# Attention values of branch A at other weight units, and transposed probabilities in six places instead of four, in a two-layer encoder on one core

## Chip, cores and metric

The kernel runs on one core of a Trainium2 chip. The metric is the device time of one execution in microseconds (us); the time of a kernel is the median over several executions. The core has five engines that run their own instruction streams and meet only through semaphores: TensorE (PE), VectorE (DVE), ScalarE (ACT), GpSimd (POOL) and SyncE (SP), which here only issues DMAs.

## What is computed

Two layers over 256 tokens of width 1024. In each, one projection `z` feeds three branches, whose gated sum passes `w_out`; then comes a SwiGLU channel mixer.

```python
h = rms_norm(x, norm_mix[l]);  z = h @ w_in[l]            # 6656 columns: qkv of A, qkv of B, pool channels, gates
ya = dense_gqa_blocked(qa, ka, va) @ w_branch_a[l]         # A: 8 query heads, softmax(q k^T) v over 256 keys
...
yb = ob.reshape(b, s, B_OUT_WIDTH) @ w_branch_b[l]         # B: 3 groups of 4 heads, windows of their own
yc = multiscale_pool(uc, pool_lin[l], pool_scale[l]) @ w_branch_c[l]   # C: pooling, then a linear map per group
merged = gates[:, :, 0] * ya + gates[:, :, 1] * yb + gates[:, :, 2] * yc
x = x + merged @ w_out[l]
x = x + (silu(h2 @ w_ffn_gate[l]) * (h2 @ w_ffn_up[l])) @ w_ffn_down[l]
```

## The kernel before

**Units.** All weights come as one stream of 68 units per layer, each 128 x 2048 float32 (1 MB), in a ring of four slots. Unit `t` is loaded into `w_raw` by SP once unit `t-4` is done, ACT rounds it to `w_hi` (line 751), DVE makes the rest `w_lo = w_raw - w_hi` (line 998), both two units ahead, and PE multiplies three passes: hi x hi (1319), hi x lo (1321), lo x hi (1330). Each pass is 128 x 512, four K tiles, for the two token halves m = 0 and 1, so an ordinary unit is 24 matmuls.

**What lies in front of a unit.** Units 0 to 25 are the projection, two units to a chunk of 512 columns (`z0` to `z12`). In front of a unit's matmuls PE may have other work: scores of two pairs of heads (lines 1410 and 1419) at units 10, 14, 18 and 22, and values, that is probabilities times v (line 1442), at 16, 20, 24 and 28. In the text, "pair p" is the p-th pair of the 16 softmax tiles, p = 0 to 7; values q takes pairs 2q and 2q+1; values 0 and 1 are branch A and end in banks `o0` and `o1`. Within a unit, between m = 0 and m = 1, come `pool` (1380) and the map of branch C, `mixed` (1386).

**PSUM banks.** Chunks `z7` to `z12` all use bank 0 for m = 0 and bank 1 for m = 1. The first matmul of the next chunk, at the even units 16, 18, 20, 22 and 24, therefore waits until DVE has taken the former chunk out of its bank. That is `take_gates` (line 1173, two instructions, m = 0 first), in DVE's program at the odd units 15 to 25. At 15 and 17 (`GATES_FIRST`) it stands ahead of the split of a weight unit, at the others behind it and behind the turns of that unit:

```python
if t in GATES_FIRST:
    take_gates(lay, t)
for j in splits_at(t):
    split(lay, j)
...
if t not in TURNS_FIRST:
    turns(lay, turns_within(t))
```

**The way of the probabilities.** ACT's exp and DVE's normalization make a pair; one unit later ACT splits them into halves (821), SP issues two DMA transposes (567) and, two units after that, POOL joins the halves (656) into `probsT` or `late_probs` (in the room of `rope`), where PE reads them. SP's program has the transposes of pair p ahead of a load of `w_raw`, and each of them waits for a join of pair p-1 (`probs_joined`). ACT's program at a unit is: split of a weight unit, split of probabilities, exp, join of heads (836, `JOINS_BEHIND`), turns (784 rounds an output `o` of values; DVE's 1053 makes its low part).

The engines have no scheduler: each stream is the order in which the loops over `t` are written, driven by these tables.

Of the kernel before, what the change touches and what calls it, by code (L numbers as in the profile page):

```python
# [31 lines left out]
NC = 512  # L32
# [9 lines left out]
RING = 4  # L42
# [10 lines left out]
UNITS = U_DOWN + 11  # L53
# [28 lines left out]
TURNED = len(REGIONS) * MT  # L82

JOINS_AHEAD = {8: [(1, 0), (1, 1)], 13: [(3, 0)]}
JOINS_BEHIND = {7: [(0, 0)], 10: [(0, 1)], 14: [(2, 0)], 15: [(4, 0)], 16: [(4, 1), (5, 0)], 17: [(3, 1)],
                18: [(2, 1), (5, 1)]}
JOIN_ORDER = [j for t in range(7, 19) for j in JOINS_AHEAD.get(t, []) + JOINS_BEHIND.get(t, [])]


# [27 lines left out]

TURNS_WITHIN = {
    0: [("mix_x", 2), ("mix_x", 3)],
    16: [("pool", 0)], 17: [("o", 0)], 18: [("pool", 1)], 20: [("o", 1)], 21: [("mixed", 0)], 23: [("mixed", 1)],  # L120
    24: [("o", 2)], 28: [("o", 3)], 30: [("merged", 0), ("merged", 1)],
    U_OUT + 3: [("ffn_x", 0), ("ffn_x", 1)], 
}

# [12 lines left out]
def quad_at(t, late):  # L137

    q, rest = divmod(t - PAIR_UNIT - late, 4)
    return q if 0 <= q < PAIRS // 2 and not rest else None  # L140
# [19 lines left out]

def turns_by_dma(t, lay=0):
    return [] if t == U_DOWN + 8 and lay == DEPTH - 1 else TURNS_BY_DMA.get(t, [])


def turns_before(t, lay=0):
# [91 lines left out]
def build(nc, x, stream, params, b_gate, eye, angles, pooling, mask, counts, out):  # L257
# [3 lines left out]
    with ExitStack() as ctx:  # L261
# [162 lines left out]
        def wait_joined(eng, lay, head):  # L424

            eng.wait_ge(heads_joined, lay * TURNED + JOIN_ORDER.index(head) + 1)
# [47 lines left out]

        def joined_probs(i):

            if i % 4 < 2:
                return probsT[:, i % 2, :]
            return late_probs[:, i % 2, :]

        def probs_part(i, j):

# [124 lines left out]
        def _(pool):  # L607
# [40 lines left out]
            def join_probs(lay, t, i):  # L648

                pool.wait_ge(probs_turned[i % 2], 16 * (lay * PAIRS + i // 2 + 1))  # L650
                if i == 2:
                    pool.wait_ge(rotated, (lay + 1) * TURNED)
                if i >= 4:
                    pool.wait_ge(unit_done, lay * UNITS + RING + t)
                both = joined_probs(i).bitcast(U16).rearrange("p (t h) -> p h t", h=2)
                nc.gpsimd.tensor_copy(both, probs_room(i).rearrange("p (h t) -> p h t", h=2)
                                      ).then_inc(probs_joined, 1)
# [644 lines left out]
        def _(pe):  # L1302
# [160 lines left out]
            for lay in range(DEPTH):  # L1463
                for t in range(UNITS):
# [3 lines left out]
                    if q is not None:  # L1468
                        scores(lay, 2 * q)
                        scores(lay, 2 * q + 1)  # L1470
                    q = quad_at(t, 6)
                    if q is not None:
                        values(lay, 2 * q)
                        values(lay, 2 * q + 1)
# [156 lines left out]
```

## Time and profile before

| | |
|---|---|
| Median of 3 runs | 802.65 us (802.24 to 803.89) |
| The profiled execution: its time / span of its trace | 802.35 / 800.5 us |
| PE busy | 794.4 us, 99% of the span |
| DVE / ACT / POOL busy | 72% / 61% / 29% |
| Granted TensorE clock over the span | 1.0 of full speed |
| Chain that ended last | 98% PE |

Times in the trace are counted from the start of the span. A row of the timeline is one instruction or several alike in a row: start, duration, engine, line, what it writes and reads, how many, and in brackets how long the engine was idle before it and what released it. A 128x512 matmul shows 0.39 us from start to end but the next one starts 0.23 us later, since they overlap; so starts are compared, not durations. The fp32 matmuls of scores, values and `mixed` appear as two records each. SPq is SP's DMA queue.

### The profile page before, as it was taken

Reading aid. Unit: us, or ns where it says so; the run is one execution under the profiler, and the core shown is the slowest. Engines: PE = TensorE matmul, PEld = TensorE weight load, DVE = VectorE, ACT = ScalarE, POOL = GpSimd, SP = SyncE. Lnnn points to the kernel's source line nnn. Section 1 sums busy time; section 2 is a strip of 40 time slices with the busy share of each in tenths; the row PEclk is TensorE's granted clock in tenths of the full one; section 3 lists DMA queues with packets and bytes.
Section 4 is the critical chain, followed back from the end, with each engine's and each line's share of the span. In section 5 each row is a group of like instructions: output and inputs, shape, how many; then the busy total and the mean of one; then the engine's idle time right before and its main releaser. Section 6 shows DMA issues by size and latency. Waiting matters only on the chain.

```text
span 800.5 us, 9766 instructions
## 1 busy us (share of the span) xinstructions
PE 794.4 (99%) x3768; PEld 652.1 (81%) x3768; DVE 579.5 (72%) x692; ACT 485.4 (61%) x554; POOL 234.4 (29%) x212
## 2 busy tenths in 40 slices
PE   8999999999999999999999999999999999999998
PEld 6888877888888888888888887878888888888886
DVE  6899977868676767655379989777686676676551
ACT  6778787673675445545557888866647645545420
POOL 1346622230014444430023316222200244444200
PEclk9999999999999999999999999999999999999999
DMA  9796898764677667676656887875746776687551
GB/s 335 287 249 200 212 257 245 211 224 165 205 235 226 201 223 215 207 254 207 202 197 195 235 220 217 251 237 180 233 169 198 233 239 201 219 233 217 195 209 50
DMA packets 109166, 173.89 MB, mean 217 GB/s; under 512 B 88608, under 2 KB 88768, under 8 KB 91712
## 3 DMA queue, kind: packets, MB, share of 16 engines
q1 hardware_dynamic: 106912, 165.96, 67.1%
q0 software_dynamic: 1920, 7.23, 2.6%
q8 instruction: 30, 0.49, 0.2%
q14 instruction: 16, 0.13, 0.1%
q10 hardware_dynamic: 288, 0.08, 0.0%
HBM read 150.96 MB, written 1.05 MB: 190 GB/s over the span
## 4 chain that ended last, share of the span: by engine, by line
PE 98%; DMA 1%; DVE 0%; ACT 0%; SPq 0%; issue 0%
PE bank L1319 31%; PE bank L1330 31%; PE bank L1321 31%; PE bank L1442 2%; PE bank L1419 1%; PE bank L1410 1%; PE bank L1352 1%; DMA x_sb<-in_x_dram 1%; PE bank L1380 0%; PE bank L1386 0%; DVE w_lo L998 0%; ACT w_hi L751 0%; ACT aT_hi L766 0%; PE bank L1452 0%; DVE scratch L1035 0%; DVE x_sb L1214 0%
## 5 line engine op out<-in xcount | busy, mean ns | idle before, releaser
L998 DVE TENSOR_TENSOR w_lo<-w_raw,w_hi 128x2048 fp32r<-128x2048 f32 x134 | 314.0, 2346 | 116.0 <-ACT w_hi L751 115.8
L751 ACT ACTIVATE w_hi<-w_raw 128x2048 fp32r<-128x2048 f32 x134 | 256.4, 1916 | 151.8 <-DMA w_raw<-in_stream_dram 151.7
L1319 PE MATMUL bank<-w_hi,aT_hi 128*128 128x512 f32 x832 | 326.6, 392 | 0.2 <-issue 0.2
L1321 PE MATMUL bank<-w_hi,aT_lo 128*128 128x512 f32 x832 | 324.1, 390 | 0.0
L1330 PE MATMUL bank<-w_lo,aT_hi 128*128 128x512 f32 x832 | 223.1, 390 | 0.2 <-DVE w_lo L998 0.2
L1319 PEld LDWEIGHTS bank<-w_hi,aT_hi 128*128 128x128 f32 x832 | 156.2, 188 | 36.6 <-issue 3.4
L1330 PEld LDWEIGHTS bank<-w_lo,aT_hi 128*128 128x128 f32 x832 | 155.7, 188 | 33.1 <-DVE w_lo L998 0.7
L1321 PEld LDWEIGHTS bank<-w_hi,aT_lo 128*128 128x128 f32 x832 | 156.2, 188 | 32.0
L680 POOL COPY halves<-hid 128x512 uint16<-128x512 uint16 x44 | 72.3, 1673 | 13.0 <-DVE hid L1291 13.0
L689 POOL COPY hT_raw<-turned 128x512 uint16<-128x512 uint16 x44 | 33.6, 809 | 124.1 <-DMA turned<-halves 124.1
L1319 PE MATMUL bank<-w_hi,hT_hi 128*128 128x512 f32 x176 | 68.5, 389 | 0.0
L1321 PE MATMUL bank<-w_hi,hT_lo 128*128 128x512 f32 x176 | 68.5, 389 | 0.0
L979 ACT ACTIVATE sg<-bank,rstd 128x256 f32<-128x256 f32 x44 | 20.8, 474 | 66.8 <-PE bank L1330 66.7
L1330 PE MATMUL bank<-w_lo,hT_hi 128*128 128x512 f32 x176 | 47.7, 389 | 0.0
L633 POOL TENSOR_TENSOR sx<-ssx 128x2 f32<-128x2 f32 x4 | 1.0, 255 | 158.5 <-ACT probsT L887 158.5
L1284 DVE SCALAR_TENSOR_TENSOR scratch<-bank,rstd,sg 128x256 f32<-128x256 f32 x44 | 20.9, 480 | 30.3 <-ACT sg L979 30.2
L1319 PEld LDWEIGHTS bank<-w_hi,hT_hi 128*128 128x128 f32 x176 | 33.0, 188 | 6.8
L1321 PEld LDWEIGHTS bank<-w_hi,hT_lo 128*128 128x128 f32 x176 | 33.0, 188 | 6.9
L1330 PEld LDWEIGHTS bank<-w_lo,hT_hi 128*128 128x128 f32 x176 | 33.0, 188 | 6.9
L629 POOL TENSOR_TENSOR rs<-rs_in,neg_half 128x8 f32<-128x8 f32 (+2 forms) x24 | 34.3, 1430 | 2.0
L627 POOL TENSOR_SCALAR rs_in<-ss 128x8 f32<-128x8 f32 (+2 forms) x24 | 8.5, 353 | 77.2 <-DVE ss L1089 76.6
L1048 DVE TENSOR_TENSOR hT_lo<-hT_raw,hT_hi 128x512 fp32r<-128x512 f32 x22 | 22.9, 1042 | 8.2 <-ACT hT_hi L771 8.2
(118 smaller groups left out, 807.6 us busy)
## 6 DMA issues: line engine op xcount, KB each, us to landing
w_raw<-in_stream_dram SPq DMA_DIRECT2D x135, 1024.0 KB, 5.0
bias_sb<-in_b_gate_dram POOLq DMA_DIRECT2D x12, 256.0 KB, 4.8
par<-in_params_dram POOLq DMA_DIRECT2D x3, 384.0 KB, 5.4
w_raw<-in_stream_dram SPq DMA_DIRECT2D x4, 256.0 KB, 5.0
head_halves<-in_pooling_dram POOLq DMA_DIRECT2D x1, 1024.0 KB, 6.1
zqk<-in_counts_dram POOLq DMA_DIRECT2D x2, 512.0 KB, 4.5
out_dram<-x_sb SPq DMA_DIRECT2D x4, 256.0 KB, 4.2
x_sb<-in_x_dram SPq DMA_DIRECT2D x2, 256.0 KB, 4.4
```

The lines of the kernel that those rows point to most:

```text
L629: nc.gpsimd.tensor_tensor(dst[0], dst[1], dst[2], ALU.pow).then_inc(signal, 1)
L680: nc.gpsimd.tensor_copy(halves[:, b, :, h, :], both[:, :, :, h]).then_inc(halves_ready, 1)
L689: nc.gpsimd.tensor_copy(both[:, :, :, :, h], turned[:, b, :, h, :, :].rearrange("p m k t -> p k m t")).then_inc(raw_ready, 1)
L751: nc.scalar.activation(w_hi[:, j % RING, :, :].rearrange("p k n -> p (k n)"), w_raw[:, j % RING, :, :].rearrange("p k n -> p (k n)"), ACT. ...
L979: nc.scalar.activation(sg[:, i % 2, m, :], B((f"f{i}", m))[:, 0:256], ACT.Sigmoid, scale=rstd[:, 1, m:m + 1]).then_inc(sig_done, 1)
L998: nc.vector.tensor_tensor(w[0], w[1], w[2].bitcast(F32), ALU.subtract).then_inc(unit_lo, 1)
L1048: nc.vector.tensor_tensor(turn_dest(name, False), raw, hi, ALU.subtract).then_inc(hidden_ready, 1)
L1284: made.append(link(nc.vector.scalar_tensor_tensor(scratch[:, 2 * NC + 256 * m:2 * NC + 256 * m + 256], B((f"f{i}", m))[:, 0:256], rstd[:, ...
L1319: nc.tensor.matmul(o, src[0][:, k, tok], w_hi[:, slot, wk + i, :], start=first and i == 0, stop=False)
L1321: nc.tensor.matmul(o, src[1][:, k, tok], w_hi[:, slot, wk + i, :], start=False, stop=False)
L1330: last = nc.tensor.matmul(o, src[0][:, k, tok], w_lo[:, slot, wk + i, :], start=False, stop=final and i == len(tiles) - 1)
L1442: last = nc.tensor.matmul(B(("o", o))[HD * r:HD * r + HD, at:at + w], zvu[:, kt, col(r):col(r) + HD], joined_probs(2 * p + r)[:, c:c + cw] ...
```

## The change

Values 0 and 1 move on PE from units 16 and 20 to 18 and 22, behind the scores there; values 2 and 3 stay. The turns of `o0` and `o1` move from 17 and 20 to 19 and 22, those of `mixed` from 21 and 23 to 23 and 24. The joined probabilities get a third room (pairs 2 and 5) in `zqk[:, 1, 0:1024]`, whose heads must have been joined by ACT first; for that, the join of heads (2, 1) moves on ACT from unit 18 to 17. POOL's join of a pair no longer waits for the end of the unit before it, but for the values that last read the room, and for pair 2 for the joins of heads (3, 1) and (2, 1).

```diff
-JOINS_BEHIND = {7: [(0, 0)], 10: [(0, 1)], 14: [(2, 0)], 15: [(4, 0)], 16: [(4, 1), (5, 0)], 17: [(3, 1)],
-                18: [(2, 1), (5, 1)]}
+JOINS_BEHIND = {7: [(0, 0)], 10: [(0, 1)], 14: [(2, 0)], 15: [(4, 0)], 16: [(4, 1), (5, 0)], 17: [(3, 1), (2, 1)],
+                18: [(5, 1)]}
...
-    16: [("pool", 0)], 17: [("o", 0)], 18: [("pool", 1)], 20: [("o", 1)], 21: [("mixed", 0)], 23: [("mixed", 1)],
-    24: [("o", 2)], 28: [("o", 3)], 30: [("merged", 0), ("merged", 1)],
+    16: [("pool", 0)], 18: [("pool", 1)], 19: [("o", 0)], 22: [("o", 1)], 23: [("mixed", 0)],
+    24: [("o", 2), ("mixed", 1)], 28: [("o", 3)], 30: [("merged", 0), ("merged", 1)],
...
+def values_at(t):
+
+    return {18: 0, 22: 1, 24: 2, 28: 3}.get(t)
...
-            if i % 4 < 2:
-                return probsT[:, i % 2, :]
-            return late_probs[:, i % 2, :]
+            room = i // 2 % 3
+            if room == 2:
+                return zqk[:, 1, NC * (i % 2):NC * (i % 2) + NC]
+            return (probsT, late_probs)[room][:, i % 2, :]
...
-                if i >= 4:
-                    pool.wait_ge(unit_done, lay * UNITS + RING + t)
+                if i in (4, 5):
+                    wait_joined(pool, lay, (3, 1))
+                    wait_joined(pool, lay, (2, 1))
+                if i >= 6:
+                    wait_full(pool, lay, ("o", (i // 2 - 3) // 2))
...
-                    q = quad_at(t, 6)
+                    q = values_at(t)
```

**PE where unit 20 begins.** The rows are the last passes of unit 19 (bank 1) and the first of unit 20 (bank 0, chunk `z10`). Before:

```order
L1319 MATMUL bank1<-w_hi,aT_hi 128x512
L1321 MATMUL bank1<-w_hi,aT_lo 128x512
L1330 MATMUL bank1<-w_lo,aT_hi 128x512 x4
L1442 MATMUL bank3<-probsT,zvu 64x256 x4
L1442 MATMUL bank3<-rope,zvu 64x256 x4
L1319 MATMUL bank0<-w_hi,aT_hi 128x512
L1321 MATMUL bank0<-w_hi,aT_lo 128x512
```

And with the change:

```order
L1328 MATMUL bank1<-w_hi,aT_hi 128x512
L1330 MATMUL bank1<-w_hi,aT_lo 128x512
L1339 MATMUL bank1<-w_lo,aT_hi 128x512 x4
L1328 MATMUL bank0<-w_hi,aT_hi 128x512
L1330 MATMUL bank0<-w_hi,aT_lo 128x512
```

The eight matmuls of values are gone from between the units; the same has happened where unit 16 begins.

**DVE from unit 17 to unit 20.** The `gates` rows are `take_gates`, the `w_lo` rows the splits of units 19, 20, 21. Before:

```order
L1173 SCALAR_TENSOR_TENSOR gates<-bank,rstd,bias_sb 128x512 x2
L998 TENSOR_TENSOR w_lo<-w_raw,w_hi 128x2048
L1053 TENSOR_TENSOR oT_lo<-bank,oT_hi 128x4x128
...
L998 TENSOR_TENSOR w_lo<-w_raw,w_hi 128x2048
...
L998 TENSOR_TENSOR w_lo<-w_raw,w_hi 128x2048
L1173 SCALAR_TENSOR_TENSOR gates<-bank,rstd,bias_sb 128x512 x2
```

With the change:

```order
L1182 SCALAR_TENSOR_TENSOR gates<-bank,rstd,bias_sb 128x512 x2
L1007 TENSOR_TENSOR w_lo<-w_raw,w_hi 128x2048
...
L1007 TENSOR_TENSOR w_lo<-w_raw,w_hi 128x2048
...
L1007 TENSOR_TENSOR w_lo<-w_raw,w_hi 128x2048
L1062 TENSOR_TENSOR oT_lo<-bank,oT_hi 128x4x128
L1182 SCALAR_TENSOR_TENSOR gates<-bank,rstd,bias_sb 128x512 x2
```

The low part of `o0` has moved between the split of unit 21 and the gates of chunk `z9`.

**ACT at units 17 to 19.** `w_hi` rows are the splits of units 19, 20 and 21, the `qkT<-zqk` rows joins of heads. Before:

```order
L751 ACTIVATE w_hi<-w_raw 128x2048
L821 ACTIVATE scratch<-probs 128x1024 x2
L836 ACTIVATE qkT<-zqk 128x2x4x128
L784 ACTIVATE oT_hi<-bank 128x4x128
L751 ACTIVATE w_hi<-w_raw 128x2048
L809 ACTIVATE probs,den<-probs,neg_max 128x512 x2
L836 ACTIVATE qkT<-zqk 128x2x2x128 x2
L789 ACTIVATE pooledT<-bank 128x512
L751 ACTIVATE w_hi<-w_raw 128x2048
L821 ACTIVATE qkT<-probs 128x1024 x2
```

With the change:

```order
L760 ACTIVATE w_hi<-w_raw 128x2048
L830 ACTIVATE scratch<-probs 128x1024 x2
L845 ACTIVATE qkT<-zqk 128x2x4x128
L845 ACTIVATE qkT<-zqk 128x2x2x128
L760 ACTIVATE w_hi<-w_raw 128x2048
L818 ACTIVATE probs,den<-probs,neg_max 128x512 x2
L845 ACTIVATE qkT<-zqk 128x2x2x128
L798 ACTIVATE pooledT<-bank 128x512
L760 ACTIVATE w_hi<-w_raw 128x2048
L830 ACTIVATE qkT<-probs 128x1024 x2
L793 ACTIVATE oT_hi<-bank 128x4x128
```

The second join, that of heads (2, 1), has come to unit 17, and the rounding of `o0` stands behind the split of pair 4 at unit 19.

## Rows read from the trace of the kernel before

**Rows 1.** The page, busy time (us), share of the span and instructions

```profile
PE 794.4 (99%) x3768; PEld 652.1 (81%) x3768; DVE 579.5 (72%) x692; ACT 485.4 (61%) x554; POOL 234.4 (29%) x212
```

**Rows 2.** Waits of PE: us in total, times, longest us

```profile
PE bank L1330 <- DVE w_lo L998: 0.2, 1, 0.2
```

**Rows 3.** Timeline of PE, layer 0, units 15 to 17

```profile
101.03 1.07 PE L1330 MATMUL bank<-w_lo,aT_hi 128*128 128x512 f32 x4
102.03 1.08 PE L1442 MATMUL bank<-probsT,zvu 128*64 128x256 f32 x8
...
103.91 0.50 PE L1319 MATMUL bank<-w_hi,aT_hi 128*128 128x512 f32 x1
...
109.55 1.07 PE L1330 MATMUL bank<-w_lo,aT_hi 128*128 128x512 f32 x4
110.46 0.39 PE L1319 MATMUL bank<-w_hi,aT_hi 128*128 128x512 f32 x1
```

**Rows 4.** Timeline of DVE, the gates of z7 in layers 0 and 1

```profile
102.03 1.40 DVE L1173 SCALAR_TENSOR_TENSOR gates<-bank,rstd,bias_sb 128x512 f32<-128x512 f32 x2
...
495.65 1.40 DVE L1173 SCALAR_TENSOR_TENSOR gates<-bank,rstd,bias_sb 128x512 f32<-128x512 f32 x2
```

**Rows 5.** Timeline of PE, layer 0, end of unit 19 and start of 20

```profile
129.03 1.07 PE L1330 MATMUL bank<-w_lo,aT_hi 128*128 128x512 f32 x4
130.03 1.08 PE L1442 MATMUL bank<-probsT,zvu 128*64 128x256 f32 x8
...
131.91 0.50 PE L1319 MATMUL bank<-w_hi,aT_hi 128*128 128x512 f32 x1
```

**Rows 6.** Timeline of DVE, layer 0: low part of o0, split of unit 21, gates of z9

```profile
120.10 0.69 DVE L1053 TENSOR_TENSOR oT_lo<-bank,oT_hi 128x512 fp32r<-128x512 f32 x1 [0.92 <-ACT oT_hi L784]
...
128.57 2.29 DVE L998 TENSOR_TENSOR w_lo<-w_raw,w_hi 128x2048 fp32r<-128x2048 f32 x1 [2.14 <-ACT w_hi L751]
130.78 1.41 DVE L1173 SCALAR_TENSOR_TENSOR gates<-bank,rstd,bias_sb 128x512 f32<-128x512 f32 x2
```

**Rows 7.** Timeline of ACT: layer 0, units 17 to 19; layer 1, units 14 to 19

```profile
114.56 1.92 ACT L751 ACTIVATE w_hi<-w_raw 128x2048 fp32r<-128x2048 f32 x1 [0.53 <-DMA w_raw<-in_stream_dram]
...
118.27 1.36 ACT L836 ACTIVATE qkT<-zqk 128x1024 uint16<-128x1024 uint16 x1
119.49 0.58 ACT L784 ACTIVATE oT_hi<-bank 128x512 fp32r<-128x512 f32 x1
...
126.62 1.92 ACT L751 ACTIVATE w_hi<-w_raw 128x2048 fp32r<-128x2048 f32 x1 [1.59 <-DMA w_raw<-in_stream_dram]
...
490.03 0.80 ACT L836 ACTIVATE qkT<-zqk 128x512 uint16<-128x512 uint16 x1
...
511.03 0.57 ACT L784 ACTIVATE oT_hi<-bank 128x512 fp32r<-128x512 f32 x1
...
519.73 1.92 ACT L751 ACTIVATE w_hi<-w_raw 128x2048 fp32r<-128x2048 f32 x1 [2.43 <-DMA w_raw<-in_stream_dram]
```

**Rows 8.** POOL's joins of probabilities: ns min/median/max, first and last start

```profile
L656 POOL COPY probsT<-zqk x8: 1359/1367/3060, 137.8 to 562.0; 128x1024 uint16<-128x1024 uint16 x8
```

**Rows 9.** Timeline of SP's queue: first transpose of pair 3, layers 0 and 1

```profile
117.44 1.24 SPq L567 DMA_TRANSPOSE gates<-scratch  x1
...
508.99 1.23 SPq L567 DMA_TRANSPOSE gates<-scratch  x1
```

**Rows 10.** Timeline of PE, layer 1, the last passes of units 15 and 19

```profile
494.77 1.07 PE L1330 MATMUL bank<-w_lo,aT_hi 128*128 128x512 f32 x4
...
522.77 1.07 PE L1330 MATMUL bank<-w_lo,aT_hi 128*128 128x512 f32 x4
```

**Rows 11.** Windows: us, PE busy (x), ..., granted clock, DMA share, GB/s; first two: warm-up matmuls

```profile
2.90:3.40 0.50, 0.50 (x7) 0.50 (x7) 1.00 0.67 182
...
7.40:7.90 0.50, 0.50 (x12) 0.50 (x10) 1.00 0.84 217
...
797.00:800.50 3.50, 0.13 (x1) 0.00 (x0) 0.69 (x1) 0.00 (x0) 0.00 (x0) 0.96 0.19 75
```

## The prediction, on record before the change ran

> **What bounds the kernel now.** I read the page first: PE is busy for 794.4 of 800.5 us [rows 1]. Then the waits of PE: none in the body is over 0.2 us [rows 2]. So PE is the bound from end to end, and every microsecond that PE waits or works more is added to the time. A change pays only through work of PE; it costs wherever it uncovers a wait that is hidden now. So I went through the timelines at the places where the change alters what PE has in front of a unit, and asked each time who must have finished.
>
> Ordinary passage between units: the four last passes start at 109.55 and the next unit starts 0.91 us later [rows 3], 0.2275 a pass. With values in front of unit 16, its first matmul starts at 103.91 instead of 101.03 + 0.91 = 101.94: values take 1.97 us [rows 3]. At unit 20 it is 131.91 against 129.94, the same [rows 5].
>
> **The change on PE.** It has the same matmuls. In each layer values 0 and 1 now stand behind scores, twice, so instead of two inserts with an entry and an exit each there is one longer insert. The 16 records of values need 16 x 0.114 (half of a 512-column pass) = 1.82 us, so 0.15 of the 1.97 is entry and exit; the entry alone is 0.09 (101.94 to 102.03). A merge saves nothing at the least, and at most both inserts' 0.15, 0.3 in all. I take 0.1 for each of the four merges, since scores and values still differ in tile shape and there is one change between them: **-0.4 us** (0 to -1.2). The Trainium skill has a rule for this (TensorEngine Tiling (Array Packing), Key Properties): changing the tiling mode drains the engine, using another tile of the same mode doesn't. By it a merge removes one of four drains, by the trace's 0.09 at entry about 0.1 each, which is what I took.
>
> **What the values covered.** Chunks z7 to z12 share banks 0 and 1, so an even unit can't start until DVE has taken the former chunk's m = 0 out of bank 0. Where values or scores stand in front, PE has 2 us of other work meanwhile. The change takes that cover from units 16 and 20 and doubles it at 18 and 22, where it is not needed.
>
> *Unit 16.* DVE takes z7 at 102.03 in layer 0 and 495.65 in layer 1, two instructions in 1.40 us, the first done after about 0.70 [rows 4]: 102.73 and 496.35. DVE's program up to there is untouched. PE is ready at 101.94 and at 494.77 + 0.91 = 495.68 [rows 10]. Waits: 0.79 and 0.67, **+1.5 us**. Behind it on PE is everything.
>
> *Unit 20.* DVE takes z9 at 130.78, right behind the split of unit 21, which starts at 128.57 because that unit's weights came late (ACT idle 1.59 for a DMA, DVE 2.14 for ACT) [rows 6, 7]. Now values at 130.03 to 131.91 hide it [rows 5]. With the change PE wants bank 0 at 129.94 + 0.79 - 0.1 = 130.63, and three things stand in the way:
>
> 1. The gates stay behind the split of 21 (19 is not in GATES_FIRST).
> 2. The turn of o0 has moved in between. ACT rounds o0 at unit 19 behind the split of pair 4: from the start of a w_hi to the end of that split are 118.27 - 114.56 = 3.71, the turn is 0.58 [rows 7], DVE's low part 0.69 [rows 6], the first gates 0.70. So bank 0 is free 3.71 + 0.58 + 0.69 + 0.70 = 5.68 us after the weights of unit 21 land.
> 3. Those weights land later. On SP the load of unit 21 is queued behind the transposes of pair 3, and these wait for the join of pair 2. That join now waits for ACT's join of heads (2, 1), which comes behind that of (3, 1): it starts where the turn of o0 started, 119.49, and takes the 0.80 of its size: 120.29 [rows 7]. One join of probabilities by POOL is 1.36 [rows 8]: 121.65. Now the first transpose starts at 117.44 [rows 9], so SP is 4.2 us later, and behind it are the second transpose and the loads of units 21 and 22. From first transpose to landing were 126.62 - 117.44 = 9.18: it lands at 130.83 instead of 126.62.
>
> Bank 0 is free at 130.83 + 5.68 = 136.51, PE is ready at 130.63: **5.9 us**. In layer 1: ACT's turn starts at 511.03, + 0.80 + 1.36 = 513.19; from transpose to landing 519.73 - 508.99 = 10.74 [rows 7, 9], landing 523.93, bank free 529.61; PE is ready at 522.77 + 0.91 + 0.67 - 0.1 = 524.25 [rows 10]: **5.4 us**.
>
> *Other places.* At 18 and 22 PE has scores and values, 4 us, in front; unit 22 comes 11 us after unit 20 and its gates stand right behind the split of 23, nothing between, so I charge nothing. If the weights of 23 lag by as much as those of 21, some 2 us of cover still remain. `mixed` has the same length inside a unit as before, and what needs it, unit 26, comes over a unit later: nothing. If its turns ran into the gates of z12, C's first unit would wait, by at most the 2.3 us of a split. POOL's joins of pairs 3 to 7 lose a wait for PE; nobody on the path waits for them: nothing. The new w_lo of unit 21 is ready before PE gets there, because PE itself is held.
>
> *Clock.* At the end of the program the granted clock is 1.00 until PE has been idle for some time: PE ends 0.13 into the window from 797.0, and the mean of 0.96 over 3.5 us says the lower level (half, 1.2 of 2.4 GHz) for 0.28 us, so the clock fell about 3.1 us after the last matmul [rows 11]. Both waits at unit 20 are longer than that, and PE has no wait like them now. At the start the warm-up matmuls come 7 per half microsecond, later 12 [rows 11], so the low rate lasted there for at least the 2.5 us from 0.9 to 3.4. In low clock half of the time is lost, 1.25 us at least for a fall; a fall may also come in one wait and not the other. I take **+2 us** (0 to 4) for both layers. The skill (TensorE: Matmul & The Clock Gate, Part 1) calls the throttled state the default that activity releases, and idleness brings back; by it both waits would be followed by slow matmuls, +2.5 or more where I count 2.
>
> **Sum.** -0.4 + 1.5 + 5.9 + 5.4 + 2 = +14.4 us on the profiled execution's 802.35 (span 800.5): 816.7. The median of the runs shown is 0.3 above that execution: 817.0.
>
> **Bounds.** Low: merges save 1.2, the weights of 21 land as now (126.62 and 519.73), bank 0 free at 132.30 and 525.41, waits 1.7 and 1.2, no fall: +3.2, 805.9. High: 10.74 from transpose to landing in layer 0 too (+1.6), both joins at the 3.06 us maximum instead of 1.36 [rows 8] (+3.4), a clock fall at both (+2): 824.
>
> **Rivals.**
>
> - *Long waits and the clock falls* (my forecast): 817.0, between 814 and 821. 0.50.
> - *Long waits, the clock holds*: 815.0, between 810 and 817. For it: an idle PE of 5.4 to 5.9 us is not far above 3.1, and no row shows a fall inside the run. 0.31.
> - *Only the order on DVE counts*, the SP chain doesn't lengthen: if transposes of pair 3 really drain while loads do, the weights of 21 are as early as now. Waits 1.7 + 1.2 + 1.5, minus 0.4: +4.0, 806.6. Against it: the join of pair 2 can't start before ACT is done with (2, 1), and ACT's row has no slack there. 0.10.
> - *More than that*: a further wait appears at unit 22 or 24 because weights of 23 and 25 lag too, 822 and above. For it: every late landing delays ACT's split of the next pair, which delays the next transposes. 0.05.
> - *The other side: not slower.* The joins of pairs 3 and later are freed from the wait for a unit's end; if that let SP and so the weights run ahead, DVE would take z9 by 130.6, PE would lose only the 1.5 at unit 16, and the merges give 0.4 to 1.2 back: 802.9 to 803.7, within 0.2%. It decides at a landing of unit 21 at 130.63 - 5.68 = 124.95 or earlier, 1.7 us before today's, while the only join ahead of that load gets later. If also DVE were early at unit 16, the merges alone would be left: 801.4 to 802.6. 0.03 for no change, 0.01 for faster.
>
> **How the numbers follow.** A difference under 0.2% (1.6 us) can't be told from none here. The first two cases hold 0.81 and share the mechanism; the time is that of the likelier, 817.0. The range 809 to 822 leaves out the third case, the fourth and the last: 0.19. Slower by over 0.2%: the first four, 0.96; same 0.03; faster 0.01.
>
> **What would show it.** Timeline of PE in the changed kernel: a gap of 0.7 to 0.8 us before unit 16 and one of 5 to 6 before unit 20, in both layers, both released by DVE's gates, and none over 0.3 elsewhere. SP's queue: the first transpose of pair 3 some 4 us later than [rows 9], ACT's wait for the weights of unit 21 longer by as much. DVE's row: w_lo, oT_lo, gates in this order, with DVE idle before oT_lo for about 1.4 us. The granted clock below 1.00 in the windows behind the long gaps. The merged inserts are 0.1 shorter than the two apart. The prediction is wrong if PE's gaps at unit 20 are under 3 us, which would mean step 3 fails, or if the gap is there but the time is made up behind it: since PE never waits now, nothing could give it back.

## The result, and the profile after

The changed kernel takes 822.7 us (median of 5 runs, 820.9 to 824.1) against 803.4 (802.2 to 803.9) for the kernel before: 1.0243 times the time. Brackets behind such a ratio are its 95% interval, here [1.0232, 1.0253]. Slower was forecast, at 817.0, with a range of 809 to 822: the direction is right, and the time lies above the range. The profiled execution has a span of 820.1 us against 800.5, and all of the 19.6 us but 0.6 is time in which PE waits or runs at its lower clock.

First the page's busy times, then the waits of PE (us in total, times, longest), which answer to [rows 1] and [rows 2]:

```profile
PE 800.5 (98%) x3768; PEld 657.4 (80%) x3768; DVE 586.4 (72%) x692; ACT 485.0 (59%) x554; POOL 228.9 (28%) x212
```

```profile
PE bank L1328 <- DVE gates L1182: 14.2, 3, 7.5
```

PE has the same 3768 matmuls and 6.1 us more busy time: slower matmuls, not more of them. In the body of the kernel the waits over 0.2 us are three, all on the gates. The timeline of PE shows where (answers to [rows 5] and [rows 10]): the end of unit 19 and the first matmul of unit 20 in layer 0, then unit 15 to 16 and unit 19 to 20 in layer 1.

```profile
129.43 1.07 PE L1339 MATMUL bank<-w_lo,aT_hi 128*128 128x512 f32 x4
136.85 0.79 PE L1328 MATMUL bank<-w_hi,aT_hi 128*128 128x512 f32 x1 [6.35 <-DVE gates L1182]
...
504.38 1.07 PE L1339 MATMUL bank<-w_lo,aT_hi 128*128 128x512 f32 x4
505.84 0.50 PE L1328 MATMUL bank<-w_hi,aT_hi 128*128 128x512 f32 x1 [0.40 <-DVE gates L1182]
...
532.90 1.07 PE L1339 MATMUL bank<-w_lo,aT_hi 128*128 128x512 f32 x4
541.47 0.79 PE L1328 MATMUL bank<-w_hi,aT_hi 128*128 128x512 f32 x1 [7.49 <-DVE gates L1182]
```

Counted from the last passes with the 0.91 us of an ordinary passage, the waits before unit 20 are 136.85 - 129.43 - 0.91 = 6.5 and 7.7 us, the one before unit 16 is 0.55 in layer 1. Their cause stands in the timelines of ACT, DVE, POOL and SP of layer 0, which answer to [rows 6, 7, 9]:

```profile
116.16 1.98 ACT L845 ACTIVATE qkT<-zqk 128x1024 uint16<-128x1024 uint16 x2
...
131.12 1.91 ACT L760 ACTIVATE w_hi<-w_raw 128x2048 fp32r<-128x2048 f32 x1 [8.18 <-DMA w_raw<-in_stream_dram]
...
134.84 0.57 ACT L793 ACTIVATE oT_hi<-bank 128x512 fp32r<-128x512 f32 x1
```

```profile
133.07 2.29 DVE L1007 TENSOR_TENSOR w_lo<-w_raw,w_hi 128x2048 fp32r<-128x2048 f32 x1 [7.97 <-ACT w_hi L760]
135.44 0.69 DVE L1062 TENSOR_TENSOR oT_lo<-bank,oT_hi 128x512 fp32r<-128x512 f32 x1
136.05 1.40 DVE L1182 SCALAR_TENSOR_TENSOR gates<-bank,rstd,bias_sb 128x512 f32<-128x512 f32 x2
```

```profile
118.30 2.64 POOL L665 COPY zqk<-gates 128x1024 uint16<-128x1024 uint16 x2 [13.62 <-ACT qkT L845]
120.85 0.55 POOL L671 DMA_DIRECT2D zqk<-in_counts_dram  x1
```

```profile
119.73 2.59 SPq L573 DMA_TRANSPOSE gates<-scratch  x2
122.38 3.03 SPq L596 DMA_DIRECT2D w_raw<-in_stream_dram  x2
```

The chain is the one that was named: ACT's joins of heads, which end at 118.14, release POOL's join of pair 2 (POOL was idle for 13.62 us before it), that releases SP's transposes at 119.73, the weights of unit 21 are queued behind them, ACT and DVE stand idle for them for 8 us, and DVE splits, turns o0 and only then takes the gates that PE needs. In a row of windows stand the stretch, its length, the busy time of PE, PE's weight loads, DVE, ACT and POOL (with instructions), and then the granted clock, the last column but two:

```profile
135.00:136.00 1.00, 0.00 (x0) 0.00 (x0) 0.92 (x2) 1.00 (x2) 0.00 (x0) 0.92 0.95 218
...
137.00:142.00 5.00, 5.00 (x12) 3.93 (x13) 5.00 (x6) 1.73 (x5) 3.12 (x3) 0.50 0.84 287
142.00:143.00 1.00, 1.00 (x4) 0.76 (x4) 1.00 (x1) 0.87 (x1) 0.00 (x0) 0.67 0.10 37
538.00:539.00 1.00, 0.00 (x0) 0.00 (x0) 1.00 (x1) 1.00 (x2) 0.00 (x0) 0.81 0.00 0
539.00:545.00 6.00, 3.53 (x8) 2.81 (x9) 5.92 (x9) 4.35 (x7) 2.37 (x3) 0.50 0.77 197
545.00:546.00 1.00, 1.00 (x5) 0.78 (x4) 1.00 (x1) 0.00 (x0) 0.76 (x1) 0.78 1.02 418
```

0.92 over 135 to 136 means 0.16 us at the lower level (1.2 of 2.4 GHz), so the clock fell at 135.84; 0.67 over 142 to 143 puts its return at 142.66. In layer 1 it was low from 538.62 to 545.44. Unit 20, which takes 5.44 us at full clock, took 8.31 and 7.41: 2.9 and 2.0 us lost, which is half of the time for which the clock was still low after PE had started again.

The balance: 6.5 + 7.7 (unit 20) + 4.9 (clock) + 0.55 (unit 16) + 0.6 (a later start, unit 15's last passes start at 101.63 instead of 101.03) - 0.4 (four merges) = 19.9, against 19.6.

### The profile page after: what moved, and what is told of

The parts are those of the page before. It is cut to its first block, busy times and chain, and to the rows that moved or that the text cites. A ratio compares the mean times of both kernels' runs of the same rounds, so it can differ in the third digit from the quotient of the medians.

```text
span 820.1 us, 9766 instructions
## 1 busy us (share of the span) xinstructions
PE 800.5 (98%) x3768; PEld 657.4 (80%) x3768; DVE 586.4 (72%) x692; ACT 485.0 (59%) x554; POOL 228.9 (28%) x212
## 4 chain that ended last, share of the span: by engine, by line
PE 86%; DMA 5%; DVE 3%; ACT 2%; issue 2%; POOL 1%; SPq 1%; ACTq 0%; DVEq 0%; POOLq 0%
PE bank L1328 27%; PE bank L1330 27%; PE bank L1339 27%; DMA w_raw<-in_stream_dram 4%; PE bank L1451 2%; DVE w_lo L1007 1%; PE bank L1361 1%; PE bank L1428 1%; ACT w_hi L760 1%; SPq L573 1%; DVE probs L1168 1%; DMA x_sb<-in_x_dram 1%; POOL probsT L665 1%; ACT scratch L830 0%; ACT qkT L830 0%
## 5 line engine op out<-in xcount | busy, mean ns | idle before, releaser
L1007 DVE TENSOR_TENSOR w_lo<-w_raw,w_hi 128x2048 fp32r<-128x2048 f32 x134 | 319.1, 2384 | 118.6 <-ACT w_hi L760 118.3
L689 POOL COPY halves<-hid 128x512 uint16<-128x512 uint16 x44 | 69.0, 1599 | 13.0 <-DVE hid L1300 13.0
L698 POOL COPY hT_raw<-turned 128x512 uint16<-128x512 uint16 x44 | 35.3, 849 | 126.0 <-DMA turned<-halves 126.0
```

The costliest lines, as they stand in the source:

```text
L689: nc.gpsimd.tensor_copy(halves[:, b, :, h, :], both[:, :, :, h]).then_inc(halves_ready, 1)
L698: nc.gpsimd.tensor_copy(both[:, :, :, :, h], turned[:, b, :, h, :, :].rearrange("p m k t -> p k m t")).then_inc(raw_ready, 1)
L1007: nc.vector.tensor_tensor(w[0], w[1], w[2].bitcast(F32), ALU.subtract).then_inc(unit_lo, 1)
```

## The experiments

The kernel before, run beside them, took 802.9 us with the first four, 803.3 with the next four, 803.4 with the three after these and 802.9 with the last. The question: the forecast named two causes that work together, the order on DVE (gates behind the late split and the turn of o0) and the late weights, and a third term that follows, the clock. Which has to be undone?

**Gates ahead at unit 19.**

```diff
-GATES_FIRST = (15, 17)
+GATES_FIRST = (15, 17, 19)
```

> The changed kernel with DVE's take_gates of chunk z9 ahead of the split of unit 21 (19 added to GATES_FIRST), nothing else. Theory (PE waits at unit 20 for bank 0, which DVE empties behind a split whose weights are late): DVE reaches the gates at about 125 us of layer 0, z9's m = 0 is full at 127.6, so bank 0 is free before unit 19 ends; both waits at unit 20 (6.5 and 7.7 us) and the low clock behind them (4.8 us) go: 822.7 - 19.0 = 803.7, at most 1 us more if the split of unit 21, now behind the gates, becomes late. Rival (PE waits for the weights of unit 21 or for a join, and DVE's gates are only named by the profile): the wait moves to unit 21 or 22 and the time stays above 812.

Measured: 811.3 us, 1.0106 [1.0088, 1.0124], a miss for the theory and for the rival. The waits before unit 20 are gone, as the theory says, but PE now waits before unit 22, 1.55 us in layer 0 and 3.7 in layer 1, with a fall of the clock behind the second; 0.91 before unit 16 of layer 1 and 0.33 before unit 24 are left besides:

```profile
546.29 0.80 PE L1328 MATMUL bank<-w_hi,aT_hi 128*128 128x512 f32 x1 [3.72 <-DVE gates L1182]
```

So 11 of 19 us hang on that one place, and the same pattern waits one chunk on: the gates of z10 at unit 21, behind the split of unit 23. The "2 us of cover" that I saw at unit 22 held only as long as PE itself was held up at unit 20.

**The turn of o0 back at 20.**

```diff
-    16: [("pool", 0)], 18: [("pool", 1)], 19: [("o", 0)], 22: [("o", 1)], 23: [("mixed", 0)],
+    16: [("pool", 0)], 18: [("pool", 1)], 20: [("o", 0)], 22: [("o", 1)], 23: [("mixed", 0)],
```

> The changed kernel with the turn of o0 at unit 20 instead of 19, nothing else: the gates of z9 stand right behind the split of unit 21 again, as before the change. Theory: of the 6.5 and 7.7 us at unit 20 the turn made DVE idle until ACT had split pair 4 and rounded o0, and 0.69 for the low part: bank 0 is free 0.8 us earlier by the changed kernel's own rows (w_lo ends at 135.36, gates start at 136.05 and 0.61 of it is the turn), so waits of 5.8 and 6.9, the clock still falls in both: 821.5. What I wrote before counted 1.4 us of DVE idle besides; the trace shows 0.08. Rival (the turn is a main part of the wait, and the clock holds with a shorter wait): below 817.

Measured: 822.0 us, 1.0238 [1.0221, 1.0255], near what was expected, with waits of 6.2 and 7.5 instead of 5.8 and 6.9. The rows of layer 0 show the gain and why it isn't seen in the waits:

```profile
132.54 1.91 ACT L760 ACTIVATE w_hi<-w_raw 128x2048 fp32r<-128x2048 f32 x1 [8.22 <-DMA w_raw<-in_stream_dram]
```

```profile
136.69 1.40 DVE L1182 SCALAR_TENSOR_TENSOR gates<-bank,rstd,bias_sb 128x512 f32<-128x512 f32 x2
```

Bank 0 is free 136.69 + 0.70 - 132.54 = 4.85 us after the landing instead of 5.63, as expected, but this time the weights landed 0.6 us later against PE, in layer 1 0.7. So the turn ahead of the gates is the small part, 0.8 us of each wait; the split behind late weights is the large one.

**Joins of heads one unit earlier.** In the other direction, the weights: ACT joins heads (3,1) and (2,1) at unit 16, so that POOL's join, the transposes and the weights behind them come earlier.

```diff
-JOINS_BEHIND = {7: [(0, 0)], 10: [(0, 1)], 14: [(2, 0)], 15: [(4, 0)], 16: [(4, 1), (5, 0)], 17: [(3, 1), (2, 1)],
+JOINS_BEHIND = {7: [(0, 0)], 10: [(0, 1)], 14: [(2, 0)], 15: [(4, 0)], 16: [(4, 1), (5, 0), (3, 1), (2, 1)],
```

> The changed kernel with ACT's joins of heads (3, 1) and (2, 1) at unit 16, nothing else. Theory (the join of pair 2 waits for the joins of heads, SP's transposes of pair 3 for that, and the weights of unit 21 for those): POOL joins pair 2 before ACT has split pair 3, the first transpose of pair 3 starts at about 116.3 instead of 119.7 in layer 0, the weights of unit 21 land at 126.5 to 127.7 instead of 131.1; the waits at unit 20 are 2.5 to 3.1 and 3.5 to 4.5 us, the clock falls in one of them at most: 809 to 814. Rival (DMA bandwidth, not the queue order, makes the weights late): the landing stays within 1 us of 131 and the time at 821 to 823.

Measured: 810.7 us, 1.0093 [1.007, 1.0116]. The time is in the expected range, but the two waits came out otherwise than expected (3.4 and 0.9 us instead of 2.5 to 3.1 and 3.5 to 4.5). The first transpose starts at 117.61 in layer 0, 2.1 us earlier than in the changed kernel, and the weights land 2.1 us earlier; in layer 1 they land 8.3 us earlier, 3.7 us ahead of unit 19's last passes, where the kernel before has 3.0 (two rows of ACT, layers 0 and 1, and PE before unit 20 of layer 1):

```profile
129.02 1.92 ACT L760 ACTIVATE w_hi<-w_raw 128x2048 fp32r<-128x2048 f32 x1 [5.23 <-DMA w_raw<-in_stream_dram]
...
527.41 1.92 ACT L760 ACTIVATE w_hi<-w_raw 128x2048 fp32r<-128x2048 f32 x1 [2.74 <-DMA w_raw<-in_stream_dram]
```

```profile
531.15 1.07 PE L1339 MATMUL bank<-w_lo,aT_hi 128*128 128x512 f32 x4
533.14 0.50 PE L1328 MATMUL bank<-w_hi,aT_hi 128*128 128x512 f32 x1 [0.92 <-DVE gates L1182]
```

That a change of ACT's order alone gives 12 us back shows that most of the late landing comes through that join. Layer 1 shows one thing more: with weights that are on time, the gates behind the split and the turn cost 0.9 us, without any values in front of unit 20.

**The places alone.** Values and turns back where they were; the six places and the waits of POOL that go with them stay.

```diff
-return {18: 0, 22: 1, 24: 2, 28: 3}.get(t)
+return {16: 0, 20: 1, 24: 2, 28: 3}.get(t)
...
-    16: [("pool", 0)], 18: [("pool", 1)], 19: [("o", 0)], 22: [("o", 1)], 23: [("mixed", 0)],
-    24: [("o", 2), ("mixed", 1)],
+    16: [("pool", 0)], 17: [("o", 0)], 18: [("pool", 1)], 20: [("o", 1)], 21: [("mixed", 0)], 23: [("mixed", 1)],
+    24: [("o", 2)],
```

> The changed kernel with values 0 and 1 back at units 16 and 20 and the turns of o0, o1 and mixed where they were before; the six places, the changed waits of POOL and the earlier join of heads (2, 1) stay. It tells the cover from the chain. Theory (both count): PE has values in front of unit 20 again, which hides 2 us, but the weights of unit 21 still come some 4 us late through the chain of joins, so PE waits 3 to 5 us for bank 0 at unit 20, or for the join of pair 3 ahead of values 1; the wait at unit 16 is gone: 810 to 817 with the clock falling in one or both. Rival (only the position of the values matters): within 0.3% of the kernel before, 801 to 805.

Measured: 817.4 us, 1.0185 [1.017, 1.02]; the timeline of PE, layer 0:

```profile
133.50 1.08 PE L1451 MATMUL bank<-probsT,zvu 128*64 128x256 f32 x8 [1.54 <-POOL probsT L665]
...
139.29 0.80 PE L1328 MATMUL bank<-w_hi,aT_hi 128*128 128x512 f32 x1 [4.70 <-DVE gates L1182]
```

The first row is a wait of its own: values 1 wait for POOL's join of pair 3. In layer 1 there is one wait, 4.88 us before unit 20, and the clock falls in both layers. With the cover of 2 us back, the new places, with the join that has to wait for ACT, still cost 14.5 us, just above the range of the theory. Values taken away from units 16 and 20 are the smaller part of the loss, 5.3 us.

**Both repairs**, `GATES_FIRST = (15, 17, 19)` and the joins at unit 16:

> Both of the two repairs: gates of z9 ahead of the split of unit 21, and ACT's joins of heads (3, 1) and (2, 1) at unit 16. Theory (late weights of unit 21 and 23 through the chain of joins are one cause, the place of the gates behind a split the other, and each repair alone leaves the other's wait): no wait at units 20 and 22, only 0.5 to 1 us a layer at unit 16, the clock stays at 1.00, the merges give 0.4 back: 803 to 804.5, no difference to the kernel before that can be told. Rival (something else is late as well): a wait over 1 us stays and the time is above 806.

Measured: 808.7 us, 1.0055 [1.0035, 1.0074]. A miss for the theory that these two repairs are enough: PE waits 3.03 us before unit 24 and 0.57 before unit 22 in layer 0, with a fall of the clock behind the first, and 0.77 before unit 16 in layer 1.

**And the gates of z7 ahead of the pooled low halves.** The last kernel with, at unit 15 of DVE,

```diff
-                    if t == U_LOW:
-                        for m in range(MT):
-                            low_pooled(lay, m)
                     if t in GATES_FIRST:
                         take_gates(lay, t)
+                    if t == U_LOW:
+                        for m in range(MT):
+                            low_pooled(lay, m)
```

> As the kernel with both repairs, and at unit 15 DVE's gates of z7 ahead of low_pooled. Theory: z7's m = 0 is full at the middle of unit 15, DVE takes it 1.3 us earlier, so the wait at unit 16 (0.4 to 1.0 us a layer) goes: 0.5 to 1.5 us under the kernel with both repairs, 802 to 803, which the merges alone put 0.4 us below the kernel before. Rival (low_pooled, now behind the second gates and so behind the end of unit 15, makes PE wait in the pooling of unit 16): no gain over the kernel with both repairs.

Measured: 806.8 us (12 runs, 803.4 to 810.2), 1.0038 [1.0021, 1.0054], where 802 to 803 was expected. The wait before unit 16 is gone, as the theory says; one is left, 2.70 us before unit 24 of layer 0. DVE's timeline shows the pattern a third time: z11's gates at unit 23 stand behind the split of unit 25, whose weights are late, and behind the turn of `mixed` 0, which the change put at unit 23.

```profile
155.75 2.29 DVE L1007 TENSOR_TENSOR w_lo<-w_raw,w_hi 128x2048 fp32r<-128x2048 f32 x1 [3.44 <-ACT w_hi L760]
157.96 0.87 DVE L1031 SCALAR_TENSOR_TENSOR scratch<-bank,par,zqk 128x256 f32<-128x256 f32 x2
159.52 1.78 DVE L1053 TENSOR_TENSOR mixT_lo<-scratch,mixT_hi 128x512 fp32r<-128x512 f32 x1 [0.69 <-ACT mixT_hi L775]
161.23 1.40 DVE L1182 SCALAR_TENSOR_TENSOR gates<-bank,rstd,bias_sb 128x512 f32<-128x512 f32 x2
```

**Gates ahead up to unit 21, nothing else**: `GATES_FIRST = (15, 17, 19, 21)`.

> The changed kernel with take_gates ahead of the split at 15, 17, 19 and 21; the late joins stay. It tells whether late weights cost by themselves. Theory: with z9 and z10 taken ahead of the splits, PE no longer waits for bank 0 at 20 and 22, and the weights of unit 23 (low part ready at about 146.4 in layer 0, needed at 150) are late for DVE but not for PE: 803 to 805.5. Rival (late weights reach PE anyway): a wait of 1 us or more for w_hi or w_lo at unit 21 to 24, or for the gates at 24, and a time above 807.

Measured: 816.0 us, 1.0148 [1.012, 1.0176]. A clear miss: no wait before units 20 and 22, but 4.27 and 4.34 us before unit 24, with the clock falling in both layers (the row is layer 0), and 0.92 before unit 16 and 0.70 inside unit 23 in layer 1. With two places of the pattern repaired the kernel is slower than with one (811.3), since the wait that is handed on is longer and brings two falls of the clock instead of one.

```profile
163.19 0.79 PE L1328 MATMUL bank<-w_hi,aT_hi 128*128 128x512 f32 x1 [4.27 <-DVE gates L1182]
```

**The clock by itself.** The changed kernel with 42 small matmuls of no use (84 records) ahead of unit 20, so that PE is not idle while it waits.

```diff
+                    if t == 20:
+                        wait_free(pe, lay, ("o", 1))
+                        for _ in range(42):
+                            nc.tensor.matmul(B(("o", 1))[0:MT * HEADS, 0:MT * HEADS],
+                                             neg_half[:, :, :].rearrange("p m h -> p (m h)"),
+                                             neg_half[:, :, :].rearrange("p m h -> p (m h)"), start=True, stop=True)
```

> The changed kernel with 42 matmuls of 68 x 68 constants, about 0.14 us each, ahead of unit 20 into bank 3, which holds nothing then and whose content nothing reads: extra work of 5.9 us in the place of the wait of 6.5 and 7.7 us. Theory (the clock falls because PE idles, and the lower level after the wait costs 2.9 and 2.0 us): the waits for the gates shrink to about 0.6 and 1.8, the granted clock stays at 1.00, units 20 take 5.5 us again, and the kernel with 5.9 us more work a layer is 4.8 us faster than the changed one: 818. Rival (the slow matmuls after the wait have another cause, such as the DMA traffic in that stretch): the time stays at 822 to 824.

Measured: 817.4 us, 1.0164 [1.0138, 1.0191]. The timeline of PE and, behind it, the windows over both places:

```profile
131.16 5.34 PE L1483 MATMUL bank<-neg_half 128*68 128x68 f32 x84
138.40 0.50 PE L1328 MATMUL bank<-w_hi,aT_hi 128*128 128x512 f32 x1 [1.90 <-DVE gates L1182]
```

```profile
128.00:146.00 18.00, 16.10 (x132) 14.07 (x131) 11.22 (x13) 9.75 (x11) 4.49 (x4) 1.00 0.77 238
528.00:546.00 18.00, 16.97 (x136) 14.79 (x135) 11.39 (x14) 10.26 (x11) 4.50 (x4) 1.00 0.76 245
```

Unit 20 still starts late, by 138.40 - 130.26 - 0.91 = 7.2 us in layer 0 (6.5 in the changed kernel) and 6.4 in layer 1 (7.7), together 0.6 us less. The clock stays at 1.00, and the median falls by 5.3 us. The two profiled executions can be set side by side: PE's last passes come 5.1 us earlier than in the changed kernel, although this execution had started 0.8 us later (unit 15's last passes at 102.46 instead of 101.63). Of these 5.9 us, 0.6 are the earlier units 20, 0.55 is the wait before unit 16 of layer 1, which this execution doesn't have, and 4.8 are left for the clock, against the 4.9 read from the trace. So the slow matmuls behind the wait come from PE's idleness and not from what else moves there.

**The counts at unit 19.** In the kernel before, POOL issues the 512 KB load of the counts at 114.70, ahead of the transposes (117.44). In the changed kernel it follows them, at 120.85 (by 1.1 us), and moves beside them and the weights.

```diff
-                    if t == 17:
+                    if t == 19:
                         load_counts(lay)
```

> The changed kernel, with the load of the counts (and what it writes) issued by GpSimd at unit 19 instead of at unit 17. In the changed kernel that load is issued at 120.85 us in layer 0, between the transposes of pair 3 (119.73) and the landing of unit 21's weights (131.12); there the way from the transposes to the landing took 11.4 us, in the kernel before 9.2, and in layer 1 (which has the load at the same place) 10.8 against 10.7. Theory A, the load lengthens the way of the transposes and the weights in layer 0: 9.2 us again, the wait before unit 20 of layer 0 falls from 6.35 to about 4.3, the time from 822.7 to about 820.5. Theory B, the 2.2 us come from something else (what happens to be moving on the other queues): the wait stays within 0.7 of 6.35 and the time within 1 us of 822.7.

Measured: 820.0 us, 1.0203 [1.0188, 1.0219]. From SP's first transpose to the landing, layer 0:

```profile
121.08 2.59 SPq L573 DMA_TRANSPOSE gates<-scratch  x2
```

```profile
130.55 1.91 ACT L760 ACTIVATE w_hi<-w_raw 128x2048 fp32r<-128x2048 f32 x1 [6.32 <-DMA w_raw<-in_stream_dram]
```

That is 9.5 us where the changed kernel has 131.12 - 119.73 = 11.4 and the kernel before has 9.2; in layer 1 it is 9.3 against 10.8. PE's waits before unit 20 fall to 4.5 and 5.9, as the first theory says. The load of the counts, 1.1 us behind the first transpose, had cost 1.5 to 1.9 us of each landing: a DMA on POOL's queue lengthened a chain on SP's. The Trainium skill says (Trainium Kernel Development and Optimization, Key Constraints) that DMAs issued from different queues run on the same 16 engines and interleave. This run agrees.

The other kernels with the load at that place (gates ahead at 19, up to 21, at all five units of the changed kernel; the turn at 20; the places alone; the filled wait) bear it out: in their 12 layers the way took 10.5 to 12.5 us. But a load ahead of the transposes is no guarantee of the short way. The kernel before has it 2.7 us ahead in layer 0, where the way is 9.2 us, and 1.9 us ahead in layer 1, where it is 10.7; with the same order in the kernel before, below, it is 0.5 and 1.1 us ahead, and the way takes 11.1 and 10.7.

**Gates ahead at all five units.** The kernel with both repairs and the order at unit 15, and `GATES_FIRST = (15, 17, 19, 21, 23)`.

> The kernel with joins at unit 16, gates ahead of the pooled low halves at unit 15 and gates ahead of the split at units 15, 17 and 19 (806.8 us; its only wait of TensorE was 2.70 us before unit 24 of layer 0, on the gates that VectorE takes at unit 23 behind the late split of unit 25), with the gates ahead of the split at units 21 and 23 too. Theory A, the waits of TensorE come from nothing but gates behind a late split or turn, and the splits themselves have room: no wait over 0.5 us before units 16 to 26, TensorE's clock stays at 1.00, and the time is that of the kernel before, 802.5 to 804. Theory B, the splits have no room left for 1.4 us more: a wait on w_lo appears before unit 23 or 25, or on the turns before unit 24, of 1 to 4 us, and 806 to 810 us come out.

Measured: 802.6 us (12 runs, 802.2 to 804.6), 0.999 [0.9982, 0.9999]. No wait of PE over 0.2 us on anything that this change touches, clock 1.00 throughout (windows over both layers' places):

```profile
90.00:190.00 100.00, 100.00 (x546) 81.16 (x545) 72.93 (x93) 70.90 (x86) 29.98 (x22) 1.00 0.77 219
440.00:620.00 180.00, 180.00 (x911) 146.54 (x910) 147.00 (x198) 128.18 (x158) 47.48 (x37) 1.00 0.74 216
```

ACT still waits 4.70 us for the weights of unit 21 in it. The 0.1% (0.7 us) below the kernel before is of the size of the four merges (0.4 us), at the edge of what can be told.

**The same order in the kernel before.** Is the repair free by itself? The kernel before, with the gates ahead at unit 15 and at 19.

> The kernel before, values at units 16 and 20 and four places, with the gates ahead of the pooled low halves at unit 15 and ahead of the split at unit 19: the part of the repair that lies on VectorE, without the change. Theory A, the repair costs nothing itself and has nothing to gain where no gates are late (the kernel before has no wait over 0.5 us there): within 0.5 us of 803.3. Theory B, the moved splits cost something in both kernels (w_lo later before unit 21, the turns later): 804.5 to 807 us, and then a part of what is left of the loss in the repaired kernels is the repair's own.

Measured: 806.6 us, 1.004 [1.0026, 1.0053]. It costs 3.2 us there, by one wait of 1.60 us in each layer, in front of values at unit 16 (layer 1):

```profile
500.11 1.08 PE L1442 MATMUL bank<-probsT,zvu 128*64 128x256 f32 x8 [1.60 <-DVE mixT_lo L1129]
```

Values 0 at unit 16 need bank 3, which the pooled low halves at unit 15 set free. With values at unit 18 nobody waits for them so early. So my second theory was right in size and wrong in place: it is not the split but the low halves. And the order at unit 15 that helps the changed kernel is one that the kernel before could not have had for nothing.

**One line.** The changed kernel with `GATES_FIRST = (15, 17, 19, 21, 23)` and nothing else.

> The changed kernel with one line altered: gates ahead of the split at units 15, 17, 19, 21 and 23. The joins stay at units 16 and 17, so the weights of unit 21 still land late (ScalarE waited 8.2 and 8.1 us for them), and at unit 15 the pooled low halves stay ahead of the gates. With the gates ahead at units 15 to 21 alone it was 816.0, with waits of 4.27 and 4.34 us before unit 24, 0.92 before unit 16 of layer 1 and 0.70 before the insert of unit 23. Theory A, only the place of the gates on VectorE matters and the late weights still come in time for the matmuls that read them: no wait before unit 24, the clock holds, about 1 us is left before unit 16 and 0 to 1 before unit 23, and the time is 803 to 805. Theory B, the late weights need the joins moved as well: a wait on w_lo, on the turns or on the gates of 2 us or more in at least one layer, and 807 to 814.

Measured: 805.6 us (12 runs, 803.9 to 809.8), 1.0042 [1.0024, 1.0059]. It is 0.6 us above the range of the first theory, and no wait is over 1.0 us. This run tells the causes apart, by one row of ACT in layer 0:

```profile
131.19 1.92 ACT L760 ACTIVATE w_hi<-w_raw 128x2048 fp32r<-128x2048 f32 x1 [8.62 <-DMA w_raw<-in_stream_dram]
```

The weights land as late as in the changed kernel (131.12), and unit 20 doesn't wait at all. What is left are 1.0 and 0.3 us before `mixed` inside unit 23, for DVE's low part of o1, and 0.67 before unit 16 of layer 1:

```profile
154.05 1.13 PE L1395 MATMUL bank<-pooledT,par 128*128 128x256 f32 x4 [1.00 <-DVE oT_lo L1062]
```

These are 2.0 us in the profiled execution, which took 804.7, 1.8 above the kernel before. The median is 2.7 above it: four of the 12 runs lie above 809, and what they waited for no profile shows.

## Where the forecast held, and the step that failed

The direction and the mechanism were forecast; the time came out 5.7 us higher, above the range, and the clock term is the largest part of that.

*PE bounds the kernel, and nothing gives a wait back*: right. Apart from 0.6 us of a later start, every microsecond of the 19.6 is a wait or lower clock.

*Merges -0.4*: right in size. In the timeline of PE the merged insert of unit 18 takes 3.92 us:

```profile
113.49 1.07 PE L1339 MATMUL bank<-w_lo,aT_hi 128*128 128x512 f32 x4
114.49 2.02 PE L1428 MATMUL bank<-qkT 64*128 64x256 f32 x24
116.44 1.08 PE L1451 MATMUL bank<-probsT,zvu 128*64 128x256 f32 x8
117.36 1.03 PE L1451 MATMUL bank<-rope,zvu 128*64 128x256 f32 x8
118.32 0.50 PE L1328 MATMUL bank<-w_hi,aT_hi 128*128 128x512 f32 x1
```

118.32 - 113.49 - 0.91 = 3.92, where values alone took 1.97 and scores alone, by the same reading at unit 18 of the kernel before, 2.05: 0.10 saved.

*Unit 16, +1.5*: too much. It waited only in layer 1, 0.55 (up to 0.96 in the other kernels with this order). In layer 0 DVE came to the gates at 101.49, when PE's last passes had started at 101.63; in [rows 3, 4] the gates start 1.0 us behind the last passes.

*Unit 20, +5.9 and +5.4*: the mechanism is right at each link, the sizes were 6.5 and 7.7. In layer 0 two errors cancelled. The first transpose came 2.3 us later and not 4.2 (119.73 against 117.44, with PE itself 0.4 later), since ACT's split of unit 19 started at 112.44 instead of 114.56, and the joins behind it with it; and the way to the landing took 11.4 instead of 9.18. That the sum fits nevertheless is luck. The second step is where a part of the change was overlooked: behind the join that now waits stands POOL's load of the counts, which the change carries from ahead of the transposes to behind them; the run with the counts at unit 19 measured it. In layer 1 the links before the chain were late too: ACT rounds the weights of unit 19 at 517.70 behind 3.02 us of waiting for them, 1.5 us later against PE than before, and everything behind shifts with it. I had taken ACT's row up to there from the kernel before. Why those weights land later in layer 1 no run shows.

The sum behind the landing (5.68) was met: 136.75 - 131.12 = 5.63. But two roads of the same length lead there. ACT is done with the turn of o0 at 134.84 + 0.57 = 135.41, DVE with the split at 133.07 + 2.29 = 135.36, and the low part starts at 135.44. DVE was idle for under 0.1 us before it, where the forecast said 1.4. Its own rows don't give 1.4 either: in [rows 6, 7] DVE's split ends 1.95 + 2.29 = 4.24 us after the landing, against 3.71 + 0.58 = 4.29 for ACT's turn.

*Clock, +2*: this is the step that failed. The term was mis-sized: it measured 4.9 by the rows and 4.8 by the filled wait, outside the 0 to 4 that was given to it. A fall was priced at 1.25 us, half of the 2.5 us of low rate among the warm-up matmuls of [rows 11] (where the granted clock column itself shows 1.00), with room for the clock to fall only once. In the changed kernel both waits had a fall, the low stretches lasted 6.8 us and not 2.5, and each cost half of what was left of it after PE started again, 2.9 and 2.0. With +4.9 in its place the sum is 819.9. The second term that was too small is the wait of layer 1, 7.7 instead of 5.4, which brings it to 822.2; the 1.0 us too much at unit 16 and the 0.6 of a later start nearly cancel.

*Other places, nothing charged*: wrong in a way that the changed kernel hides. Units 22 and 24 have no wait there because unit 20 has one. Once that is removed, the wait appears at 22, then at 24 (the runs with the gates ahead at 19, with both repairs, and with the gates ahead up to 21). The rival "more than that" named the places, but saw them as further waits, not as the same one handed on.

*Rivals*: "only the order on DVE counts" fell on SP's row in the changed kernel, as argued. Yet the last run shows a truth beside it: the order on DVE is what turns late weights into a wait of PE. The large waits need both. Late weights with the gates ahead cost 2.7 us, late weights with the gates behind 19.3; and weights on time with the gates behind cost 0.9 us in layer 1 of the kernel with the joins at unit 16.

## What to carry to other kernels

When an engine's program mixes work that waits for a DMA with work that frees a bank, put what frees the bank first at every place of the pattern, not at the first one that shows a wait: here repairing one handed the wait to the next, and only with the fifth entry of the table was this kernel back. When a join or copy is moved, list every DMA issued behind it on its own queue too, since it may move from ahead of a critical transfer to beside it, and compare how long the same way took in every layer and kernel on record: it was 8.3 to 13.0 us here. For an engine with a clock that falls, take a wait's price as the wait plus half of the low stretch that outlasts it, at each place.

## What the runs showed of the hardware

The clock fell at different times and, mostly, for the same length. After idle times of 6.35, 7.49 and 3.41 us the low level lasted 6.8 us each time, and so it did after eight more waits of 3.7 to 6.2 us in the other runs. It was 10.2 us after the wait of 7.45 us (turn at 20, layer 1) and 3.4 after those of 2.70 and 3.03. For the wait of 3.41 us (joins one unit earlier) the windows read:

```profile
130.00:135.00 5.00, 1.59 (x7) 1.01 (x7) 3.95 (x4) 5.00 (x5) 0.00 (x0) 0.84 0.58 174
135.00:142.00 7.00, 7.00 (x21) 5.49 (x22) 6.96 (x9) 3.55 (x6) 3.12 (x3) 0.63 0.64 206
```

That is 5 x 0.16 / 0.5 = 1.6 us low in the first and 7 x 0.37 / 0.5 = 5.2 in the second, so the clock fell near 133.4, some 2 us after PE's last matmul ended (131.3), where the changed kernel shows 5.3 and 4.7 us. And a wait of 2.70 us, before unit 24 in the kernel with the gates of z7 ahead of the low halves, was followed by a fall 1.1 us after PE had started again (162.02), low for 3.4 us:

```profile
163.00:164.00 1.00, 1.00 (x4) 0.76 (x4) 1.00 (x5) 0.74 (x3) 0.00 (x0) 0.58 0.99 418
164.00:166.00 2.00, 2.00 (x7) 1.54 (x6) 2.00 (x2) 1.05 (x4) 0.00 (x0) 0.50 0.05 21
166.00:167.00 1.00, 1.00 (x5) 0.86 (x4) 0.93 (x5) 0.00 (x0) 0.00 (x0) 0.72 0.00 0
```

The wait of 3.03 us had its fall 1.0 us after PE had started again, too. So the wait's length alone doesn't say how much the clock takes: the wait of 3.41 us had 5.4 us of low clock behind it (134.75 to 140.2), the one of 2.70 us 3.4, and waits of 1.55, 1.60 and 1.90 had none.
